# Differential attention scores from stacked high and low parts, second-map scaling on GpSimd, turned heads by transfers, and unread products in TensorE's waits

## The chip, the cores and the metric

One program runs on one core of a Trainium2 chip. The metric is the device time of one execution, in microseconds (us). The engines are named as the profile names them: PE is TensorE's products (PEld its weight loads), DVE is VectorE, ACT is ScalarE, POOL is GpSimd, SP is SyncE, which here only issues transfers. A q behind an engine's name is its sequencer.

## What is computed

Two transformer blocks over 512 tokens of 1024 features, with a small context of 256 tokens in the second. The first block has sliding-window attention with a pooled mixer, and a retrieval layer (PEER) over 16,384 experts. The second has two layers: differential attention with a SwiGLU feed-forward, then a short convolution with another. The change lies almost wholly in the differential attention, whose core is, for each of 8 heads with two maps each:

```
q, k = rope(rmsnorm(h @ wq)), rope(rmsnorm(h @ wk))   # 64 features per map; context keys without rope
s[m] = q[m] @ k[m].T / 8                              # two maps, 512 queries, 512 + 256 keys
p[m] = softmax(s[m])
o    = (p[0] - lam * p[1]) @ v                        # then an rmsnorm over 128 features, then w_o
```

rope's rotated copy exchanges neighbouring blocks of 16 features (`-x2, x1, -x4, x3`).

## The kernel before, in words

All weights pass through SBUF in units of 128x1024, in a ring of 8 slots: SP loads a unit (`load_unit`, L458), ACT writes its rounded high part (`split_hi`, L1147), POOL writes the rest as low part in four pieces of 256 columns (`low_part`, L535 to L540), and PE makes each fp32 product from three single-pass products (high by high, high by low, low by high: L639 to L641). Elsewhere, where both operands are plain fp32, one product takes two PE instructions. Every engine's work is written out in order by hand, with semaphores between engines, so the order of instructions in each engine's block is the schedule.

The stages around the change, in time order (the span starts at 0):

- Queries and keys, 1550 to 1683 us. For each of 16 own heads (8 of keys `Kd`, 8 of queries `Qd`, each 128 rows for two maps' halves) PE makes a unit's 24 products, ACT squares and copies the bank (`evict`, L1446), PE sums the squares (`head_squares`, L918), and PE turns the copy by a product with a 128x128 matrix (`rotate`, L926). DVE then runs `own_head` (L2104): turned times sine (L2111), straight times cosine and gain (L2112), their sum (L2113), a reciprocal of the root (L2102), a scaling (L2115). Four context items of keys lie between. ACT may run four items ahead of DVE.
- Values, 1681 to 1757 us: four pairs of value units, six products' groups each; the first two rounds' scores are put into the last pair.
- The rounds, 1757 to 1908 us: 32 rounds of one head and 128 queries. In round a PE makes the scores of round a + 2 (`at_scores`, L998, 64 rows by 128 queries by 512 and 256 keys, for two maps that lie in different halves of the rows), transposes round a (L1009) and multiplies values of the head before (L1018). DVE finds the maxima (`at_max`, L2131), ACT takes the exponentials with their sums (`at_exps`, L1499), DVE inverts the sums (`at_parts`, L2152, L2153), ACT scales the second map by -lam over its sum (`at_second`, L1505), DVE adds the first map to it (`at_combine`, L2158), PE transposes, ACT copies (L1542). Within DVE's round the order is `at_parts(a+1)`, two `at_max(a+2)`, `at_combine(a+1)`, then a head's odd work (L2164 on, L2186). One bank pair per map holds the scores, so scores wait for the exponentials of the round before. During these rounds POOL has nothing to do, and the first units of the output projection lie ready in the ring.
- The output projection from 1911 us, the first feed-forward to 2324 us, the convolution's norm (L1132) with PE waiting for DVE, and the rest to the end.

## Time and profile before

| | |
|---|---|
| median of 3 runs | 2876.49 us (2873.24 to 2891.11) |
| the profiled execution | 2884.48 us, of which the span of instructions is 2882.7 us |
| mean granted TensorE clock of the profiled execution | 0.992 |
| PE busy | 2806.1 us, 97% of the span |
| DVE, ACT, POOL busy | 1779.1, 982.2, 1611.1 us |

The span is what the rows below refer to; the execution has 1.8 us around it. PE is busy nearly throughout, but busy time is counted from each product's start to its modelled end, and products overlap, so a share near 1 does not say that products follow as fast as they can.

### The profile page before, as it was taken

What the parts mean: (1) busy time and instruction counts of PE and PEld (TensorE: products, weight loads), DVE (VectorE), ACT (ScalarE), POOL (GpSimd) and SP (SyncE); (2) the same over time, 40 slices, a digit from 0 to 9 for tenths busy, and PEclk for the clock granted to TensorE, in tenths of its full rate; (3) what the DMA queues carried; (4) which work ended last, traced back from release to release, by engine and by line L of the source; (5) the groups of instructions that cost most, each with busy time, mean ns of one, the idle gap of its engine ahead of it and who ended that gap; (6) DMA issues with size and microseconds to landing.
All of it is one profiled execution on the core that took longest, in us unless ns stands there. A gap on an engine that the chain in (4) does not pass through costs nothing.

```text
span 2882.7 us, 39051 instructions
## 1 busy us (share of the span) xinstructions
PE 2806.1 (97%) x14400; PEld 2399.9 (83%) x14400; DVE 1779.1 (62%) x2749; ACT 982.2 (34%) x1452; POOL 1611.1 (56%) x1649
## 2 busy tenths in 40 slices
PE   8799999999999999999999999999999989999999
PEld 6698888888888899999998786579888868988887
DVE  6668999997652378788887855754333353433333
ACT  4432333322223333333334446843122232332121
POOL 5444878787777357878741441016455545555543
PEclk9999999999999999999999999999999999999999
DMA  6932444489984699999993111003222222222221
GB/s 200 342 140 82 145 145 148 140 327 320 331 289 155 230 320 336 337 353 348 368 353 110 59 59 48 1 20 109 102 95 100 97 73 97 94 95 95 88 103 72
DMA packets 191668, 499.23 MB, mean 173 GB/s; under 512 B 29624, under 2 KB 80952, under 8 KB 190904
## 3 DMA queue, kind: packets, MB, share of 16 engines
q1 hardware_dynamic: 104528, 338.95, 33.8%
q10 hardware_dynamic: 52200, 91.23, 9.0%
q0 software_dynamic: 34816, 67.41, 6.6%
q8 instruction: 76, 1.25, 0.2%
q14 instruction: 48, 0.39, 0.0%
HBM read 432.82 MB, written 64.68 MB: 173 GB/s over the span
## 4 chain that ended last, share of the span: by engine, by line
PE 86%; POOL 5%; DVE 3%; DMA 2%; issue 2%; ACT 1%; SPq 0%; ACTq 0%; DVEq 0%
PE ps L639 27%; PE ps L641 26%; PE ps L640 26%; POOL value_rows L566 2%; POOL picked L558 2%; PE ps L998 2%; PE ps L1018 1%; DMA unit_raw<-w_units 1%; PE ps L1009 1%; DMA value_rows<-w_units,row_at 1%; PE ps L918 1%; PE ps L828 0%; PE ps L926 0%; DMA abuf<-act_dram 0%; DVE std L1624 0%
## 5 line engine op out<-in xcount | busy, mean ns | idle before, releaser
L540 POOL TENSOR_TENSOR unit_lo<-unit_raw,unit_hi 128x256 fp32r<-128x256 f32 x984 | 761.9, 811 | 939.0 <-ACT unit_hi L1155 938.4
L639 PE MATMUL ps<-hn_hi,unit_hi 128*128 128x512 f32 (+1 forms) x2352 | 910.8, 387 | 23.6 <-DVE hn_lo L1725 11.7
L640 PE MATMUL ps<-hn_lo,unit_hi 128*128 128x512 f32 (+1 forms) x2352 | 896.3, 381 | 0.0
L641 PE MATMUL ps<-hn_hi,unit_lo 128*128 128x512 f32 (+1 forms) x2352 | 896.3, 381 | 0.0
L1155 ACT ACTIVATE unit_hi<-unit_raw 128x1024 fp32r<-128x1024 f32 x486 | 506.0, 1055 | 459.4 <-DMA unit_raw<-w_units 359.7
L639 PEld LDWEIGHTS ps<-hn_hi,unit_hi 128*128 128x128 f32 x2352 | 443.1, 188 | 124.2 <-issue 14.5
L572 POOL DMA_INDIRECT gate_dram<-gate_sums,gate_at x384 | 468.6, 1220 | 136.9 <-issue 126.7
L640 PEld LDWEIGHTS ps<-hn_lo,unit_hi 128*128 128x128 f32 x2352 | 443.3, 188 | 87.1 <-issue 4.5
L641 PEld LDWEIGHTS ps<-hn_hi,unit_lo 128*128 128x128 f32 x2352 | 443.1, 188 | 85.2
L1857 DVE TENSOR_TENSOR unit_lo<-unit_raw,unit_hi 128x1024 fp32r<-128x1024 f32 x240 | 292.3, 1222 | 107.8 <-ACT unit_hi L1155 104.8
L639 PE MATMUL ps<-gp_hi,unit_hi 128*128 128x384 f32 x1024 | 345.5, 337 | 12.5 <-DVE gp_lo L2019 12.5
L641 PE MATMUL ps<-gp_hi,unit_lo 128*128 128x384 f32 x1024 | 344.1, 336 | 0.0
L640 PE MATMUL ps<-gp_lo,unit_hi 128*128 128x384 f32 x1024 | 343.9, 336 | 0.0
L2241 DVE TENSOR_TENSOR pf<-gel,ps 128x512 f32<-128x512 f32 x44 | 30.3, 688 | 379.7 <-PE ps L641 379.7
L1356 ACT ACTIVATE stage<-ps 128x512 f32<-128x512 f32 x128 | 76.6, 599 | 492.7 <-PE ps L641 492.7
L566 POOL DMA_INDIRECT value_rows<-w_units,row_at x128 | 188.0, 1469 | 100.6 <-DVE own_values L2037 60.5
L558 POOL DMA_INDIRECT picked<-act_dram,act_at x128 | 177.6, 1387 | 67.8 <-issue 38.7
L639 PEld LDWEIGHTS ps<-gp_hi,unit_hi 128*128 128x128 f32 x1024 | 193.8, 189 | 15.2 <-DVE gp_lo L2019 10.8
L1575 ACT ACTIVATE gel<-ps 128x512 f32<-128x512 f32 x44 | 26.4, 599 | 497.2 <-PE ps L641 497.2
L640 PEld LDWEIGHTS ps<-gp_lo,unit_hi 128*128 128x128 f32 x1024 | 193.8, 189 | 0.0
L641 PEld LDWEIGHTS ps<-gp_hi,unit_lo 128*128 128x128 f32 x1024 | 193.5, 189 | 0.0
L2037 DVE SCALAR_TENSOR_TENSOR own_values<-value_rows,picked,own_values 128x1024 f32<-128x1024 f32 x127 | 163.0, 1284 | 42.3 <-DMA value_rows<-w_units,row_at 40.2
(284 smaller groups left out, 3784.3 us busy)
## 6 DMA issues: line engine op xcount, KB each, us to landing
unit_raw<-w_units SPq DMA_DIRECT2D x486, 512.0 KB, 3.6
araw<-ada_units SPq DMA_DIRECT2D x96, 512.0 KB, 6.0
act_dram<-stage ACTq DMA_DIRECT2D x32, 1024.0 KB, 6.6
gate_dram<-zero SPq DMA_DIRECT2D x8, 3072.0 KB, 24.7
abuf<-act_dram ACTq DMA_DIRECT2D x32, 768.0 KB, 7.9
gbuf<-gate_dram ACTq DMA_DIRECT2D x15, 1536.0 KB, 21.2
gate_dram<-gate_sums,gate_at POOLq DMA_INDIRECT x384
x<-x_t SPq DMA_DIRECT2D x8, 256.0 KB, 6.4
```

The lines of the kernel that those rows point to most:

```text
L540: last = nc.gpsimd.tensor_tensor(lo[:, u % RING, cols], raw[:, u % RING, cols], hi[:, u % RING, cols].bitcast(F32), ALU.subtract)
L558: pool.indirect_dma_start(picked[:, k:k + 1], None, act_dram.rearrange("u j (t o) -> (u j t) o", o=1), bass.IndirectOffsetOnAxis(act_at[:, ...
L566: pool.indirect_dma_start(vrows[:, k % ROWS, :], None, w_units.rearrange("u p n -> (u p) n"), bass.IndirectOffsetOnAxis(row_at[:, k:k + 1] ...
L572: pool.indirect_dma_start(gate_dram.rearrange("i j (t o) -> (i j t) o", o=1), bass.IndirectOffsetOnAxis(gidx[:, t - 1, k:k + 1], 0), gsum[ ...
L639: mm(dst, wh, ah, start=start, stop=False)
L640: mm(dst, wh, al, start=False, stop=False)
L641: return mm(dst, wl, ah, start=False, stop=stop)
L998: last = mm(SD[m][:, keys], Qd[rows, 4 * m + h // 2, qt * P:(qt + 1) * P], Kd[rows, 4 * m + h // 2, keys], start=True, stop=True)
L1155: activation(hi[:, u % RING], raw[:, u % RING], ACT.Copy).then_inc(hi_ready, 1)
L1356: activation(stage[:, g % 2, u % BUNCH], ps[:, u % 4, :], ACT.Gelu).then_inc(gel_done, 1)
L1857: V.tensor_tensor(lo[:, u % RING], raw[:, u % RING], hi[:, u % RING].bitcast(F32), ALU.subtract).then_inc(value_lo_ready, 1)
L2037: last = V.scalar_tensor_tensor(own[:, :], vrows[:, k % ROWS, :], picked[:, k:k + 1], own[:, :], ALU.mult, ALU.add)
```

## The change

Seven edits:

1. `rotate` goes from PE. SP copies each evicted head's blocks of 16 rows into another buffer, exchanged, by 8 transfers of 16x512 (`turn_head`), and DVE's first step takes that buffer from SBUF with gain and signed sine (the sign now lies in the sine table). Items may run six ahead of DVE instead of four.
2. Scores are made from rounded parts. Per head and map ACT writes the high part of keys and queries (`high_keys`, `high_queries`); POOL writes the keys' low part into the other 64 rows, a second copy of the queries' high part into the other 64, and the queries' low part. One product of 128 rows and one of 64, both single-pass, then take the place of each fp32 product of 64 rows. Heads 0 and 1 are prepared during the values, the others during the rounds, two ahead.
3. `at_second` moves from ACT to POOL.
4. The parts lie in ring slots, so the output units load later: three after the scores of the sixth head, the others after all scores; their high and low parts are put into the last rounds and behind.
5. `keep_clock` issues products nobody reads: 9 ahead of the rounds, 3 in each of the first four rounds, 11 and 26 around the convolution's norm.
6. The load of x is waited for in three groups instead of eight pieces.
7. Buffers are moved to make room; the turning matrix leaves the constants.

```diff
 CTX_SQUARE = 112
+TURN = [(p + 16) % 32 for p in range(32)]
+X_GROUPS = (2, 3, 3)
...
         def pooled_bank(g):
             return ps[:, 4 if g == 3 else 5 + g, :]
+        def head_rows(h, m):
+            b = (h + m) % 2
+            return slice(64 * b, 64 * b + 64), slice(64 - 64 * b, 128 - 64 * b)
+        def key_parts(h, m):
+            return keyp[h // 2 % 2][:, 2 * (h % 2) + m, :]
+        def query_parts(h, m):
+            return qryp[h // 2 % 2][:, 4 * (h % 2) + m, :]
+        def query_low(h, m):
+            return qryp[h // 2 % 2][:, 2 + m, :]
         def seam_bank(k, j):
...
+        PARTS_AFTER = {0: (unit_used, U_DIFF + 2 * DC + 2), 1: (unit_used, U_DIFF + 2 * DC + 4),
+                       2: (unit_used, U_DIFF + 2 * DC + 6), 3: (unit_used, U_DIFF + 2 * DC + 6),
+                       4: (at_s, 2 * 2 * TT), 5: (at_s, 2 * 2 * TT), 6: (at_s, 4 * 2 * TT), 7: (at_s, 4 * 2 * TT)}
...
+                sp.wait_ge(hd_ev, upto("own", m))
+                if m == 0:
+                    sp.wait_ge(x_spilled, 16)
+                if m >= len(turnb):
+                    sp.wait_ge(hd_done, upto("own", m - len(turnb)))
+                for a in range(0, P, 32):
+                    for to, of in ((a, a + 16), (a + 16, a)):
+                        sp.dma_start(turnb[k][to:to + 16, :], src[of:of + 16]).then_inc(turn_in[k], 16)
             for n in range(2 * DC):
                 load_unit(U_DIFF + DC + n, of=U_DIFF + DC + (n + DC) % (2 * DC))
-            load_range(U_DIFF + 3 * DC, N_UNITS)
+                turn_head(n)
+            for n in range(DC):
+                if n == 0:
+                    sp.wait_ge(at_s, 6 * 2 * TT)
+                elif n == 3:
+                    sp.wait_ge(at_s, 8 * 2 * TT)
+                load_unit(U_WO + n)
+            load_range(U_WO + DC, N_UNITS)
             for c in range(DC):
                 sp.wait_ge(x_done, X_ALL - DC + c + 1)
...
+            def low_keys(h, m):
+                pool.wait_ge(head_high, 2 * h + 1)
+                own, other = head_rows(h, m)
+                summed(G_.tensor_tensor(key_parts(h, m)[other], Kd[own, 4 * m + h // 2, :],
+                                        key_parts(h, m)[own].bitcast(F32), ALU.subtract))
+            def high_again(h, m):
+                pool.wait_ge(head_high, 2 * h + 2)
+                own, other = head_rows(h, m)
+                summed(G_.tensor_copy(query_parts(h, m)[other], query_parts(h, m)[own].bitcast(F32)))
+            def low_queries(h, m):
+                own, _ = head_rows(h, m)
+                summed(G_.tensor_tensor(query_low(h, m)[own], Qd[own, 4 * m + h // 2, :],
+                                        query_parts(h, m)[own].bitcast(F32), ALU.subtract))
+                if m:
+                    G_.sem_inc(parted, 1)
+            def at_second(a):
+                pool.wait_ge(at_m, 3 * a + 3)
+                G_.tensor_scalar(Ed[a % 3][:, 1, :], Ed[a % 3][:, 1, :], stats[:, a % 2, 1, 3:4], None, ALU.mult)\
+                    .then_inc(at_scaled, 1)
+                pool.wait_ge(at_scaled, a + 1)
+            pool.wait_ge(lo_ready, U_PEER + LOW_FROM + U_WO - (U_DIFF + LAG))
+            for h in range(2):
+                for m in range(2):
+                    low_keys(h, m)
+                for m in range(2):
+                    high_again(h, m)
+                for m in range(2):
+                    low_queries(h, m)
+            at_second(0)
+            at_second(1)
+            for a in range(TT * HEADS):
+                if a + 2 < TT * HEADS:
+                    at_second(a + 2)
+                h, step = 2 + a // 4, a % 4
+                if h < HEADS:
+                    if step < 2:
+                        low_keys(h, step)
+                    elif step == 2:
+                        for m in range(2):
+                            high_again(h, m)
+                    else:
+                        for m in range(2):
+                            low_queries(h, m)
+                if 26 <= a < 29:
+                    low_part(U_WO + a - 26)
+            low_range(U_WO + 3, N_UNITS)
...
                 last.then_inc(unit_used, 1)
+            def keep_clock(u, bank, n):
+                s = u % RING
...
                     if a:
-                        pe.wait_ge(at_exp, 3 * (a - 1) + m + 1)
-                    rows = slice(64 * ((h + m) % 2), 64 * ((h + m) % 2) + 64)
+                        pe.wait_ge(at_exp, 2 * (a - 1) + m + 1)
+                    own, _ = head_rows(h, m)
                     for keys in (slice(0, T), slice(T, KEYS)):
-                        last = mm(SD[m][:, keys], Qd[rows, 4 * m + h // 2, qt * P:(qt + 1) * P],
-                                  Kd[rows, 4 * m + h // 2, keys], start=True, stop=True)
+                        mm(SD[m][:, keys], query_parts(h, m)[:, tok], key_parts(h, m)[:, keys], start=True, stop=False)
+                        last = mm(SD[m][:, keys], query_low(h, m)[own, tok], key_parts(h, m)[own, keys], start=False,
+                                  stop=True)
                     last.then_inc(at_s, 1)
...
             pe.wait_ge(v_ev, KTS * DC // 2)
+            keep_clock(U_WO - 1, 7, 9)
             for a in range(N_AT):
                 h, qt = a // TT, a % TT
                 if a + 2 < N_AT:
                     at_scores(a + 2)
                 at_transpose(a)
+                if h == 0:
+                    keep_clock(U_WO - 1, 7, 3)
                 if h and qt < 3:
                     at_values(h - 1, (2 * qt, 2 * qt + 1))
                 if h >= 2 and qt == 1:
...
+            unit_in(U_SC)
+            keep_clock(U_SC, 3, 11)
             norm(5)
+            keep_clock(U_SC, 3, 26)
             for j in range(DC):
                 if j >= 2:
...
-                    act.wait_ge(hd_done, i - 3)
+                if i >= len(nb):
+                    act.wait_ge(hd_done, i - len(nb) + 1)
...
+            def high_keys(h):
+                act.wait_ge(hd_done, upto("own", DC // 2 + h // 2))
+                act.wait_ge(*PARTS_AFTER[h])
+                for m in range(2):
+                    own, _ = head_rows(h, m)
+                    last = activation(key_parts(h, m)[own], Kd[own, 4 * m + h // 2, :], ACT.Copy)
+                last.then_inc(head_high, 1)
+            def high_queries(h):
+                act.wait_ge(hd_done, upto("own", DC + DC // 2 + h // 2))
+                for m in range(2):
+                    own, _ = head_rows(h, m)
+                    last = activation(query_parts(h, m)[own], Qd[own, 4 * m + h // 2, :], ACT.Copy)
+                last.then_inc(head_high, 1)
             for s in range(2 * DC):
...
+                    if n in (2, 4) and t == 0:
+                        act.wait_ge(hd_done, upto("own", 2 * DC - 3))
                     activation(Vd[n][:, t, :], ps[:, 6 + j % 2, 0:P], ACT.Copy)
                     activation(Vd[n + 1][:, t, :], ps[:, 6 + j % 2, P:2 * P], ACT.Copy).then_inc(v_ev, 1)
                     if t == 0:
                         behind_unit(2 * DC + n)
+                    if n in (2, 4) and t == 1:
+                        high_keys(n // 2 - 1)
+                        high_queries(n // 2 - 1)
+                    if n == DC - 2 and t == 2:
+                        high_keys(2)
                     if n == DC - 2 and t == 1:
                         at_exps(0)
-                    if n == DC - 2 and t == 3:
-                        at_second(0)
                 behind_unit(2 * DC + n + 1)
             at_exps(1)
-            at_second(1)
             for a in range(N_AT):
...
                 if h % 2 and h >= 3 and qt == 1:
                     at_roots(h - 3)
+                if qt == 1 and h + 2 < HEADS:
+                    high_queries(h + 2)
+                if qt == 3 and h + 3 < HEADS:
+                    high_keys(h + 3)
+                if 25 <= a < 28:
+                    split_hi(U_WO + a - 25)
                 if a == 2:
...
             at_roots(HEADS - 2)
+            for u in range(U_WO + 3, U_WO + AHEAD):
+                split_hi(u)
...
             def own_head(m):
                 i = upto("own", m) - 1
                 dst, g = (Kd[:, m, 0:T], pc("dk")) if m < DC else (Qd[:, m - DC, :], gain(8)[:, 0:1])
-                dve.wait_ge(hd_rot, m + 1)
+                k = m % len(turnb)
+                dve.wait_ge(turn_in[k], 128 * (m // len(turnb) + 1))
                 if i:
                     dve.wait_ge(hd_done, i)
-                V.tensor_tensor(rtmp[:, :], turn_bank(m), cs[:, 1], ALU.mult).then_inc(hd_turned, 1)
+                V.scalar_tensor_tensor(turnb[k][:, :], turnb[k][:, :], turns(m // DC), cs[:, 1], ALU.mult, ALU.mult)
                 link(V.scalar_tensor_tensor(dst, dst, g, cs[:, 0], ALU.mult, ALU.mult))
-                link(V.tensor_tensor(dst, dst, rtmp[:, :], ALU.add))
+                link(V.tensor_tensor(dst, dst, turnb[k][:, :], ALU.add))
                 head_inverse(i)
-                V.tensor_tensor(dst, dst, nb[:, i % 4, :], ALU.mult).then_inc(hd_done, 1)
+                V.tensor_tensor(dst, dst, nb[i % len(nb)][:, :], ALU.mult).then_inc(hd_done, 1)
             def context_heads(c):
...
-                dve.wait_ge(at_exp, 3 * a + 2)
+                dve.wait_ge(at_exp, 2 * a + 2)
                 link(V.reciprocal(st[:, :, 3], st[:, :, 2]))
                 V.tensor_scalar(st[:, 1, 3:4], st[:, 1, 3:4], lamt[:, 69:70], None, ALU.mult).then_inc(at_m, 1)
             def at_combine(a):
-                dve.wait_ge(at_exp, 3 * a + 3)
+                dve.wait_ge(at_scaled, a + 1)
                 V.scalar_tensor_tensor(Ed[a % 3][:, 0, :], Ed[a % 3][:, 0, :], stats[:, a % 2, 0, 3:4],
                                        Ed[a % 3][:, 1, :], ALU.mult, ALU.add).then_inc(at_p, 1)
```

## Rows read from the trace of the kernel before

**Rows 1.** The page: the span, and the chain that ended last by engine.

```profile
span 2882.7 us, 39051 instructions
...
PE 86%; POOL 5%; DVE 3%; DMA 2%; issue 2%; ACT 1%; SPq 0%; ACTq 0%; DVEq 0%
```

**Rows 2.** Windows: length, busy time of each engine, clock, DMA; queries and keys, the rounds.

```profile
core 0: us, PE busy (x) PEld busy (x) DVE busy (x) ACT busy (x) POOL busy (x), PEclk, DMA share, GB/s
1562.00:1683.00 121.00, 120.90 (x527) 90.59 (x527) 107.63 (x79) 61.92 (x96) 51.95 (x62) 1.00 0.22 73
...
1757.00:1908.00 151.00, 140.36 (x636) 81.31 (x637) 107.77 (x185) 118.94 (x204) 2.67 (x4) 0.95 0.06 21
```

**Rows 3.** Groups of PE instructions by line, 1550 to 1700 us: turning the keys.

```profile
L926 PE MATMUL ps<-Kd,rot_gains 128*128 128x512 f32 x16 | 8.2, 592 | 0.0
```

**Rows 4.** The chain in order of time: start, length, what.

```profile
1564.17 0.86 PE ps L926 x2
```

**Rows 5.** Timeline of DVE: the first own head's first step, the last one's last.

```profile
1565.17 0.69 DVE L2111 TENSOR_TENSOR rtmp<-ps,cs 128x512 f32<-128x512 f32 x1 [3.59 <-PE ps L926]
...
1695.37 0.69 DVE L2115 TENSOR_TENSOR Qd<-Qd,nb 128x512 f32<-128x512 f32 x1
```

**Rows 6.** Timeline of SP's queue at the start: issuing eight transfers.

```profile
2.13 4.88 SPq L485 DMA_DIRECT2D x<-x_t x8
```

**Rows 7.** Transfers by line: size, median us from issue to landing.

```profile
x<-x_t SPq DMA_DIRECT2D x8, 256.0 KB, 6.4
...
out_dram<-x SPq DMA_DIRECT2D x8, 256.0 KB, 2.0
```

**Rows 8.** Timeline of PE in three rounds.

```profile
1801.79 1.57 PE L998 MATMUL ps<-Kd,Qd 64*128 64x512 f32 x8
...
1804.00 1.88 PE L1018 MATMUL ps<-PTd,Vd 128*128 128x512 f32 x4
1805.81 2.11 PE L998 MATMUL ps<-Kd,Qd 64*128 64x512 f32 x8
...
1809.50 2.44 PE L998 MATMUL ps<-Kd,Qd 64*128 64x512 f32 x8 [0.78 <-ACT Ed L1499]
```

**Rows 9.** Timeline of ACT: first exponentials of rounds 2 and 31.

```profile
1761.64 0.90 ACT L1499 ACTIVATE Ed<-ps,stats 128x768 f32<-128x768 f32 x1 [1.64 <-DVE stats L2131]
...
1894.22 0.90 ACT L1499 ACTIVATE Ed<-ps,stats 128x768 f32<-128x768 f32 x1 [0.81 <-DVE stats L2131]
```

**Rows 10.** Groups of ACT instructions by line in the rounds, 1757 to 1908 us.

```profile
L1499 ACT ACTIVATE Ed<-ps,stats 128x768 f32<-128x768 f32 x62 | 55.4, 900 | 19.1 <-DVE stats L2131 19.1
L1505 ACT ACTIVATE Ed<-Ed,stats 128x768 f32<-128x768 f32 x31 | 29.1, 939 | 7.4 <-DVE stats L2153 7.4
```

**Rows 11.** Groups of DVE instructions by line in the rounds.

```profile
L2131 DVE TENSOR_REDUCE stats<-ps 128x1 f32<-128x768 f32 x60 | 55.0, 955 | 22.0 <-PE ps L998 21.9
L2158 DVE SCALAR_TENSOR_TENSOR Ed<-Ed,stats 128x768 f32<-128x768 f32 x31 | 31.3, 1009 | 1.0 <-ACT Ed L1505 1.0
L2153 DVE TENSOR_SCALAR stats<-stats,lamt 128x1 f32<-128x1 f32 x31 | 6.6, 214 | 1.1
```

**Rows 12.** Groups of POOL instructions by line, whole span.

```profile
L596 POOL TENSOR_SCALAR pool_tmp<-pool_tmp 128x496 f32<-128x496 f32 x2 | 2.9, 1456 | 0.1
L597 POOL TENSOR_TENSOR pool_p<-pool_tmp,pool_p 128x512 f32<-128x512 f32 x2 | 2.5, 1265 | 0.2
L593 POOL TENSOR_TENSOR pool_tmp<-pool_tmp 128x510 f32<-128x510 f32 x2 | 2.1, 1040 | 0.0
```

**Rows 13.** Timeline of POOL: a unit's four low pieces beside DVE's heads, and alone.

```profile
1660.68 3.87 POOL L540 TENSOR_TENSOR unit_lo<-unit_raw,unit_hi 128x256 fp32r<-128x256 f32 x4 [5.39 <-ACT unit_hi L1155]
...
1700.28 2.84 POOL L540 TENSOR_TENSOR unit_lo<-unit_raw,unit_hi 128x256 fp32r<-128x256 f32 x4 [9.91 <-ACT unit_hi L1155]
```

**Rows 14.** One line's instructions: min, median, max ns.

```profile
L2112 DVE SCALAR_TENSOR_TENSOR Qd<-Qd,gmod,cs x8: 741/936/1204, 1642.8 to 1690.5; 128x512 f32<-128x512 f32 x8
```

**Rows 15.** Windows: one in the rounds, one in the convolution's norm.

```profile
1828.00:1832.00 4.00, 4.00 (x16) 3.33 (x18) 2.68 (x4) 2.54 (x6) 0.00 (x0) 0.50 0.00 0
2330.00:2335.00 5.00, 0.42 (x1) 0.45 (x2) 4.80 (x5) 1.39 (x2) 0.00 (x0) 0.50 0.00 0
```

More of the change, by code:

```diff
@@ L99 @@
 CTX_SQUARE = 112
+TURN = [(p + 16) % 32 for p in range(32)]
+X_GROUPS = (2, 3, 3)
+X_GROUP = [k for k, n in enumerate(X_GROUPS) for _ in range(n)]
 FINAL = (6, 7, 0, 1, 2, 3, 4, 5)
@@ L277, in cc @@
             return con[:, o + a:o + a + (w - a if n is None else n)]
-        ident, blocks, ones, rot, iota = (cc(n) for n in ("ident", "blocks", "ones", "rot", "iota"))
+        ident, blocks, ones, iota = (cc(n) for n in ("ident", "blocks", "ones", "iota"))
         eps, epsd = cc("eps"), cc("epsd")
@@ L288, in gain, with turns @@
             return gmod[:, 8 * k:8 * k + 8]
+        def turns(which):
+            return gain(9)[:, 2 + which:3 + which]
         NORMS = [(x, T, pc("norm1"), None, hn_hi, hn_lo),
@@ L345, in build_program @@
         consts_in = sem("consts_in")
-        x_loaded, con2_in = [sem(f"x_loaded{c}") for c in range(DC)], sem("con2_in")
+        x_loaded, con2_in = [sem(f"x_loaded{c}") for c in range(len(X_GROUPS))], sem("con2_in")
         x_done = sem("x_done")
@@ L659, in project @@
                 last.then_inc(unit_used, 1)
+            def keep_clock(u, bank, n):
+                s = u % RING
+                for _ in range(n):
+                    mm(ps[:, bank, :], hi[:, s, 0:P], hi[:, s, 0:T], start=True, stop=True)
             def norm(k):
@@ L1045, in _ @@
                 if n == DC - 2:
-                    pe.wait_ge(hd_done, N_ITEMS)
                     at_scores(0)
@@ L1459, in evict @@
                 for to, of in moves:
-                    last = activation(nb[to, i % 4, :], ps[of, n % 2 if kind == "own" else 2 + n % 2, :], ACT.Square)
+                    last = activation(nb[i % len(nb)][to], ps[of, n % 2 if kind == "own" else 2 + n % 2, :], ACT.Square)
                 last.then_inc(hd_sq, 1)
@@ L2319, in constants @@
     put("ones", 1.0 / P)
-    turn = np.zeros((P, P))
-    for m in range(P):
-        if m % 32 < 16:
-            turn[m + 16, m] = -1.0
-        else:
-            turn[m - 16, m] = 1.0
-    put("rot", turn)
     put("iota", r[None, :])
```

63 lines of the change are left out of this document (28 added, 35 removed).

## The prediction

> **What bounds the kernel now.** I read the page first, then the windows of the stages that the change touches, then the lines and the timelines inside them. The chain that ended last lies 86% on PE [rows 1], so time is won only where PE, or what PE waits for, gets shorter. Two stages matter. In the queries and keys PE is busy 120.9 of 121 us, but DVE is busy 107.6 too, and its heads run from 1565.2 to 1696.1 us, 13 us past the end of PE's part [rows 2, 5]: DVE is the second bound, close behind. In the rounds PE is busy 140 of 151 us, ACT 119, DVE 108, POOL 2.7 [rows 2]. A round takes 4.57 us on the mean, from the first exponentials of round 2 at 1761.64 us to those of round 31 at 1894.22, over 29 rounds [rows 9]. Sometimes PE sets it (a round's scores start as soon as the values of the last are through), sometimes the ring of scores, maximum, exponentials, with PE idle before the scores (0.78 us in one row) [rows 8]. So no engine is far ahead of the others, and what a lighter PE gives there depends on which engine takes over.
>
> **The change part by part.**
>
> *Turning by transfers.* PE loses 32 instructions. A pair takes 0.86 us of the chain [rows 4] and there are 16 pairs (the row of keys has 16 instructions in 8.2 us, and the queries as many [rows 3]): 16 x 0.86 = 13.8 us less for PE. In return SP issues 8 transfers a head. Eight issues took 4.88 us [rows 6], and a landing took 2.0 us in one group and 6.4 in another, both of larger pieces [rows 7]; I take 2.5. So DVE has its first turned head about 4.9 + 2.5 us after the copy at about 1562.5, near 1570, some 5 us later than now, and 9 at the upper bound. SP's queue then holds 5 us of issues per head of 6 to 7 us, with the unit loads between; a unit load waits at most behind one head's transfers and is eight units ahead. DVE's first step becomes one of two SBUF inputs, 0.74 to 1.2 us instead of 0.69 [rows 5, 14]: 16 x 0.2 = 3 us. Against that DVE no longer waits for PE inside the stage, 11 us in 3 waits, as the first of 3.59 us shows [rows 5]; now it is behind from the start, and PE may run six items ahead. DVE therefore ends near 1570 + 126, at 1696, as now. PE reaches the values 13.8 us earlier, at about 1667, and the first thing there that wants DVE's last heads is an eviction at about 1687, for the third last head, due at about 1682. The margin is 5 us; if transfers land late it is gone and up to 5 us are given back. I take -13.8, bounds -14 and -8.
>
> *Scores.* The old products are only 64 rows high and the two maps lie in different halves of the rows. When both are free to go, eight instructions take 1.57 us, and one waiting for the other map 2.11 or 2.44 [rows 8]. The new ones fill all 128 rows, so the maps can't lie side by side. Per map there are two products over 512 and two over 256 columns, single-pass. Four 512-column products of the two-pass kind take 1.88 us [rows 8], so a map's (3 such lengths) costs at most 1.4 us, and 0.65 if a single pass runs twice as fast as half of an old one. I take 1.3 us for both maps. That is 0.3 to 1.1 us less for PE in a round, and no halving.
>
> *What POOL gets.* Per head and four rounds: four scalings of 128x768 with one input, two subtractions over 768 columns, two copies and two subtractions over 512. The one long scaling by a constant in the trace is 496 columns in 1.456 us [rows 12]; by columns 768 would be 2.25, and with a fixed start somewhat less: 2.2. Subtractions at 1.265 for 512 columns give 1.9 for 768 [rows 12]; no long copy is there, and I put it below the addition of 1.04, at 0.9. Sum: 4 x 2.2 + 2 x 1.9 + 2 x 0.9 + 2 x 1.27 = 16.9 us a head. POOL and DVE slow each other where DVE reads two SBUF inputs: four low pieces took 3.87 us beside two such steps of DVE and 2.84 alone [rows 13], about 0.5 per step, and the DVE step went from 0.74 to as much as 1.2 us [rows 14]. `at_combine` is such a step, one per round: 4 x 0.5 more. So POOL needs 18.9 us for a head, **4.75 us a round**, which is more than the 4.57 of today. It is behind a second wait too: `at_combine` waits for POOL, and queued behind it on DVE are the inversion and the maxima of the next rounds, for which ACT and then PE wait. That loop is the inversion with its scaling, 0.4 (0.214 for the second [rows 11]; the one ahead is as short), POOL 2.2, `at_combine` 1.0 alone and 1.5 beside POOL's next step [rows 11, 14], a head's odd work 0.3 to 0.6 and two handovers: 4.5 to 4.9. Both say the same.
>
> Beside a measured 2.2 us per scaling stands a page: the Trainium skill, "GPSIMD Engine Reference", 4.1 Engine selection, says that a GpSimd operation with one input runs at roughly line rate. Then 768 columns would cost below 1 us, an estimate from that page of the Trainium skill. The row here (1.456 us for 496 columns, longer than an addition of two inputs over 510) speaks against it [rows 12].
>
> *What ACT loses and gets.* It loses 0.94 us a round [rows 10] and gets, per head, two copies of 64x768 and two of 64x512: at the same 0.94 for 768 columns and about 0.6 for 512, 3.1 us a head, 0.8 a round. ACT is where it was.
>
> *The rounds, summed.* 24 rounds carry a step of the parts: 24 x 4.75 = 114.0. Three carry a low part of an output unit instead: 2.2 + 2.84 + 0.5 = 5.5 each, 16.6. Two carry neither: 0.4 + 2.2 + 1.0 + 0.6 = 4.2, 8.4. Sum 139.0 against the 132.6 of rows 9, +6.4. PE then stands idle about a sixth of a round, and where PE was held up the clock has fallen: it was at 0.50, the level of 1.2 GHz, for the window at 1828, when PE had just waited for exponentials [rows 15]. At that level four us hold two us of work. I add 4 us for two or three more such stretches (0 to 12). So +10.4.
>
> *The small ones.* Two rounds' scores among the values: -0.5. Nine unread products ahead of the rounds: at most 9 x 0.47 by the four products of rows 8, I take 2, and 2 back for a clock that stays up (0 to 3). The three per round in the first head run while PE would wait. Around the convolution's norm PE is idle anyway, 0.42 of 5 us busy at a clock of 0.50 [rows 15]; the first products behind it come at DVE's pace, so a full clock gives 0 to 1 us: 0. The late output units: three come during the rounds (counted), five after the last scores, with 25 us to the output projection (their lows at 2.84 each [rows 13] are ahead of PE): 0, and up to 3 if not. The load of x in groups: the copies that wait longer stand in front of a wait for the second unit: 0, up to 0.5.
>
> Sum: -13.8 + 10.4 - 0.5 = -3.9. Against the profiled execution's 2884.5 that is 2880.6; the median of the runs shown is 8.0 lower, and I forecast by it: 2876.5 - 3.9 = **2872.6**.
>
> **The rivals.**
>
> *POOL is quick.* If a scaling goes at the rate of the additions, 1.04 x 768 / 510 = 1.57 us [rows 12], or less, POOL needs 4 us a round at most, and ACT (two exponentials with their sums 2.0, a copy 0.8, the parts 0.8, odd work and table loads 0.5) and PE hold the round at about 4.2: 29 x 4.2 + 4 = 126, -6.8. Time 2876.5 - 13.8 - 6.8 - 0.5 = 2855. For it speaks that the long scalings of the trace are only two; against it, that both took the same 1.456 us. By the line rate of the Trainium skill the time would be this one too, since ACT and PE then hold the round.
>
> *The clock falls through the rounds: slower.* PE has about 4 us of work in a round of 4.75, and fewer in a head's last round, without values. If PE drops to 1.2 GHz in more than about 15 of the rounds, a round there takes up to 8 us at half rate; at +2.7 each on the mean, 15 rounds are +40: 2872.6 + 40 = 2913. It decides from some 13 such rounds on (35 us). For it: the window at 1828 [rows 15]. Against: the mean clock is 0.95 over the rounds although PE waits in many [rows 2].
>
> *POOL is slowed throughout.* If all POOL work pays 1.36 (3.87 over 2.84 [rows 13]), a head takes 23 us, 5.75 a round: 24 us more, 2897.
>
> *The turning is not won.* If transfers come late or DVE ends 8 us later, PE waits among the values: 2881.
>
> **How the numbers follow.** Forecast 0.45, POOL quick 0.25, clock 0.12, POOL slowed 0.10, turning not won 0.08. The range that leaves out no more than 2 in 10 goes from a quick POOL with every small bound (2855 less 6) to the slowed POOL with one stretch of low clock (2897 + 9): 2849 to 2906. Within 1% (28.8 us, about what a measurement of this kernel can tell from no change) lie 2848 to 2905. Faster by over 1% needs a POOL quicker than the quick case, and all of the clock: 0.14. Slower by over 1% is the clock case and a part of the slowed POOL: 0.14. The rest, 0.72, is within 1%.
>
> **What would show it.** The turned product gone from PE and the values starting 12 to 14 us earlier; DVE's heads ending near 1696. In the rounds POOL busy above 85% for the first 24, DVE's longest wait the one of `at_combine` for POOL, scalings of 2.2 us, and first exponentials 4.7 to 4.8 us apart. ACT and PE with more idle time than now. I am wrong if POOL's scaling is well off 2.2 us in either direction, if PE's clock is below 0.9 over the rounds, or if PE waits for DVE's evictions among the values.

## The result and the profile after

The changed kernel takes 2894.5 us (median of 20 runs, 2883.4 to 2910.7), beside 2880.3 us for the kernel before on the same chip (20 runs). The ratio, with its 95% interval, is 1.0050 [1.0033, 1.0068]: 14 us slower, where 4 us less had been forecast. The profiled execution after has a span of 2893.5 us, 10.8 more than the one before; page and windows first, which answer to [rows 1, 2].

```profile
span 2893.5 us, 39382 instructions
...
PE 84%; POOL 7%; DVE 4%; DMA 2%; issue 2%; ACT 1%; SPq 0%; POOLq 0%; ACTq 0%; DVEq 0%
```

```profile
core 0: us, PE busy (x) PEld busy (x) DVE busy (x) ACT busy (x) POOL busy (x), PEclk, DMA share, GB/s
1562.00:1683.00 121.00, 120.70 (x613) 98.26 (x611) 113.23 (x82) 65.44 (x108) 55.46 (x68) 1.00 0.36 102
1757.00:1908.00 151.00, 147.96 (x563) 83.83 (x562) 115.16 (x167) 101.87 (x180) 133.74 (x76) 0.99 0.09 33
2330.00:2345.00 15.00, 14.82 (x63) 11.40 (x62) 12.79 (x16) 6.62 (x11) 2.46 (x3) 1.00 0.19 71
```

In the rounds POOL has gone from 2.7 to 133.7 us of 151, PE from 140.4 to 148.0, and the clock is 0.99, higher than before. So PE has no more slack there than it had, although its work was to become lighter. Where the time went is read from ScalarE's timeline, first exponentials of rounds 2 and 31 (answers to [rows 9]):

```profile
1748.67 0.90 ACT L1621 ACTIVATE Ed<-ps,stats 128x768 f32<-128x768 f32 x1 [2.85 <-DVE stats L2259]
...
1901.89 0.90 ACT L1621 ACTIVATE Ed<-ps,stats 128x768 f32<-128x768 f32 x1 [3.10 <-DVE stats L2259]
```

The rounds take 1901.9 - 1748.7 = 153.2 us, 5.28 each, against 132.6 and 4.57: **20.6 us more**. They start 13.0 us earlier: 2.4 of that was there before ScalarE's first step on the queries and keys (at 1559.0 us instead of 1561.4), 12.0 come from the turning, and 1.4 are lost again among the values. Behind the rounds 3.0 us more are lost up to the first output projection product, which starts at 1921.95 us instead of 1911.27. From there to the end it is 971.6 us after and 971.4 before: -13.0 + 20.6 + 3.0 + 0.2 = +10.8, the whole difference of the spans.

Who paces the rounds? First GpSimd, its groups over 1690 to 1925 us, and then its timeline beside VectorE's in one round:

```profile
L698 POOL TENSOR_SCALAR Ed<-Ed,stats 128x768 f32<-128x768 f32 x32 | 70.5, 2204 | 45.9 <-DVE stats L2281 44.4 <-POOL query_parts L690 0.2
L678 POOL TENSOR_TENSOR key_parts<-Kd,key_parts 64x768 fp32r<-64x768 f32 x16 | 38.8, 2427 | 10.6 <-ACT key_parts L1589 9.3
L690 POOL TENSOR_TENSOR query_parts<-Qd,query_parts 64x512 fp32r<-64x512 f32 x16 | 25.4, 1589 | 1.3
...
L685 POOL CAST query_parts<-query_parts 64x512 fp32r<-64x512 f32 x16 | 13.4, 838 | 1.0
```

```profile
1829.73 2.21 POOL L698 TENSOR_SCALAR Ed<-Ed,stats 128x768 f32<-128x768 f32 x1 [0.69 <-DVE stats L2281]
1832.02 3.51 POOL L690 TENSOR_TENSOR query_parts<-Qd,query_parts 64x512 fp32r<-64x512 f32 x2
1837.16 2.20 POOL L698 TENSOR_SCALAR Ed<-Ed,stats 128x768 f32<-128x768 f32 x1 [1.64 <-DVE stats L2281]
1839.45 2.64 POOL L678 TENSOR_TENSOR key_parts<-Kd,key_parts 64x768 fp32r<-64x768 f32 x1
```

```profile
1831.97 1.02 DVE L2286 SCALAR_TENSOR_TENSOR Ed<-Ed,stats 128x768 f32<-128x768 f32 x1 [0.33 <-POOL Ed L698]
1832.91 1.50 DVE L2296 TENSOR_SCALAR ob<-Od 128x512 f32<-128x512 f32 x1
1834.44 1.64 DVE L2297 TENSOR_TENSOR ob<-ob 128x512 f32<-128x512 f32 x1
1836.00 0.74 DVE L2314 SCALAR_TENSOR_TENSOR Od<-Od,gmod,ps 128x512 f32<-128x512 f32 x1
1836.66 0.16 DVE L2280 RECIPROCAL stats<-stats 128x2 f32<-128x2 f32 x1
1836.85 0.21 DVE L2281 TENSOR_SCALAR stats<-stats,lamt 128x1 f32<-128x1 f32 x1
```

Read these as a chain: scaling, then `at_combine` 0.03 us later, then `at_square` (1.50 + 1.64 us here; 0.42 + 0.69 in the kernel before, rows below), `at_scale` (0.74 us, the norm's gain), the inversion, and only then the next scaling, for which GpSimd stands still 1.64 us. This round is 7.43 us long from scaling to scaling.

```profile
L2169 DVE TENSOR_TENSOR ob<-ob 128x512 f32<-128x512 f32 x7 | 4.8, 693 | 0.2
L2168 DVE TENSOR_SCALAR ob<-Od 128x512 f32<-128x512 f32 x7 | 3.0, 422 | 0.0
```

Now PE, one map's scores and the rest of a round (answers to [rows 8]; L1096 has 128 rows, L1097 has 64):

```profile
1776.93 0.49 PE L1096 MATMUL ps<-key_parts,query_parts 128*128 128x512 f32 x1
1777.35 0.50 PE L1097 MATMUL ps<-key_parts,query_parts 64*128 64x512 f32 x1
1777.78 0.39 PE L1096 MATMUL ps<-key_parts,query_parts 128*128 128x256 f32 x1
1778.10 0.38 PE L1097 MATMUL ps<-key_parts,query_parts 64*128 64x256 f32 x1
1778.41 0.87 PE L1108 MATMUL ps<-con,Ed 128*128 128x128 f32 x6
1779.12 1.88 PE L1117 MATMUL ps<-PTd,Vd 128*128 128x512 f32 x4
...
1783.69 0.55 PE L1108 MATMUL ps<-con,Ed 128*128 128x128 f32 x3
```

Starts are what counts, since ends are modelled. They lie 0.42 us apart at 512 columns and 0.31 at 256, so one map takes 1.48 us and both 2.96. From transposes to transposes a round with values and without a wait is 1783.69 - 1778.41 = 5.28 us on PE. That this is also the mean round is chance: the next round, a head's last, has no values and takes 3.76 us, one that carries the norm's sums takes 6.18, and from 1787.45 to 1807.96 us four rounds of PE take 20.5, 5.13 each. PE's waits from 1757 to 1908 us (us in all, how many, the longest):

```profile
PE ps L1096 <- ACT Ed L1621: 2.1, 2, 1.1
```

PE stands idle for 2.1 of the 153.2 us, so as the kernel stands PE sets the rounds. Whether GpSimd's chain would hold them as long without PE this profile can't say. So there are two candidates for the pace, and they lie on top of each other.

### The profile page after: what moved, and what is told of

Its sections match the earlier page's. It is cut to its first block, busy times and chain, and to the rows that moved or that the text cites. A ratio compares the mean times of both kernels' runs of the same rounds, so it can differ in the third digit from the quotient of the medians.

```text
span 2893.5 us, 39382 instructions
## 1 busy us (share of the span) xinstructions
PE 2836.1 (98%) x14426; PEld 2422.1 (84%) x14426; DVE 1799.2 (62%) x2751; ACT 977.9 (34%) x1452; POOL 1759.2 (61%) x1729
## 4 chain that ended last, share of the span: by engine, by line
PE 84%; POOL 7%; DVE 4%; DMA 2%; issue 2%; ACT 1%; SPq 0%; POOLq 0%; ACTq 0%; DVEq 0%
PE ps L740 27%; PE ps L742 26%; PE ps L741 26%; POOL value_rows L610 2%; POOL picked L602 2%; POOL Ed L698 1%; DMA unit_raw<-w_units 1%; DMA value_rows<-w_units,row_at 1%; PE ps L1097 1%; PE ps L1096 1%; PE ps L1025 1%; PE ps L935 0%; DMA abuf<-act_dram 0%; POOL unit_lo L584 0%; PE ps L1117 0%
## 5 line engine op out<-in xcount | busy, mean ns | idle before, releaser
L740 PE MATMUL ps<-hn_hi,unit_hi 128*128 128x512 f32 (+1 forms) x2352 | 910.2, 387 | 17.6 <-DVE hn_lo L1851 10.2
```

Of the source, the lines that this page charges most:

```text
L740: mm(dst, wh, ah, start=start, stop=False)
```

## Experiments

All ratios are to the kernel before on the same chip. The rounds are the time from the first exponentials of round 2 to those of round 31, read as above from one profiled execution of each run; PE idle and the granted clock are those of the same stretch. In these executions the first copy of a key head lies anywhere from 1546.0 to 1574.1 us, so their whole times aren't compared. The theory at the start was the prediction's own (GpSimd's loop sets the rounds); the rival was PE's products.

| run | scaling on | score products | rounds us | each | PE idle us | clock | ratio [95%] |
|---|---|---|---|---|---|---|---|
| before | ScalarE | old | 132.6 | 4.57 | 8.4 | 0.96 | 1 |
| changed | GpSimd | 128 and 64 rows in turn | 153.2 | 5.28 | 2.1 | 0.99 | 1.0050 [1.0033, 1.0068] |
| e1 | ScalarE | in turn | 158.3 | 5.46 | 2.6 | 0.96 | 1.0075 [1.0051, 1.0099] |
| e5 | GpSimd | 128 rows first | 152.1 | 5.24 | 12.2 | 0.93 | 1.0038 [1.0019, 1.0057] |
| e6 | GpSimd | both 128 rows | 151.6 | 5.23 | 30.5 | 0.95 | 1.0028 [1.0001, 1.0055] |
| e7 | GpSimd | only the 128 rows | 151.5 | 5.23 | 37.1 | 0.88 | 1.0017 [0.9995, 1.0039] |
| e8 | GpSimd | old, parts still made | 153.8 | 5.30 | 17.9 | 0.93 | 1.0022 [1.0003, 1.0042] |
| e12 | ScalarE | 128 rows first | 142.7 | 4.92 | 10.1 | 0.96 | 0.9997 [0.9972, 1.0021] |
| e9 | ScalarE | both 128 rows | 131.4 | 4.53 | 17.5 | 0.97 | 0.9945 [0.9923, 0.9967] |
| e13 | GpSimd | both 128 rows, small squares | 146.4 | 5.05 | 28.4 | 0.98 | 0.9999 [0.9980, 1.0017] |
| e15 | GpSimd | in turn, small squares | 152.7 | 5.26 | 0.0 | 0.97 | 1.0055 [1.0034, 1.0076] |
| e2 | ScalarE | old, no parts | 133.5 | 4.60 | 7.8 | 0.95 | 0.9947 [0.9925, 0.9969] |
| e10 | GpSimd | old, no parts | 129.5 | 4.47 | 6.1 | 0.98 | 0.9949 [0.9923, 0.9975] |

### The pieces by themselves

**e1, scaling back on ScalarE.**

```diff
-                G_.tensor_scalar(Ed[a % 3][:, 1, :], Ed[a % 3][:, 1, :], stats[:, a % 2, 1, 3:4], None, ALU.mult)\
-                    .then_inc(at_scaled, 1)
...
+                activation(Ed[a % 3][:, 1, :], Ed[a % 3][:, 1, :], ACT.Copy, scale=stats[:, a % 2, 1, 3:4])\
+                    .then_inc(at_scaled, 1)
```

> The changed kernel with the second map's scaling back on ACT; the parts of the scores stay on POOL. Theory A (the rounds are set by the loop from DVE's inversion over POOL's scaling and POOL's next step back to DVE): a round falls from 5.28 us to 4.3 to 4.5, some 25 us less than the changed kernel, ratio to the kernel before 0.996. Theory B (the rounds are longer because of the parts themselves, ACT's and POOL's copies and the new products; the scaling is hidden): rounds stay near 5.2, ratio 1.005.

Measured: 1.0075, rounds of 5.46 us. Its window of the rounds:

```profile
1757.00:1908.00 151.00, 148.53 (x546) 84.53 (x546) 104.20 (x162) 120.69 (x199) 53.72 (x44) 0.95 0.08 29
```

GpSimd is now 54 us busy and PE 148.5 of 151. The theory that GpSimd's loop alone makes the rounds long falls: with that loop gone, PE, idle for 2.6 us, keeps them as long. The 5.1 us over the changed kernel fit the fall of the granted clock: at the lower level, 1.2 GHz, PE takes twice as long (value products start 0.85 us apart there in e5, 0.43 at the full clock), so (1 - 0.957) x 158.3 = 6.8 us are lost here and (1 - 0.989) x 153.2 = 1.7 there, an estimate from the two clocks.

**e2, the turning alone**, put into the kernel before (with x loaded in three groups, which frees the semaphores):

```diff
-                    rotate(s - 1)
...
+                turn_head(n)
```

> The kernel before with the turning by transfers alone (and the load of x waited for in three groups). Theory A and B: the values start 12 us earlier, the rounds stay at 4.57 us, ratio 0.996. If the turning were given back among the values (late transfers, DVE behind): 0.999 to 1.000.

Measured: 0.9947, so 15 us won. **e3** is the reverse, the changed kernel with the old turning.

> The changed kernel with the turning undone (PE turns the heads again). If the turning is worth its 12 us there too: ratio 1.009. If its gain is lost behind slower rounds that do not care when they start: 1.005.

Measured: 1.0090 [1.0064, 1.0116], 12 us over the changed kernel, with the same rounds (153.5 us). By the ratios the turning is worth 12 to 15 us in either surrounding. The traces are sharper: from the first copy of a key head to the first eviction of the values it is 121.7 us in the two kernels that turn on PE (before, e3) and 109.7 in all the others, so 12.0 us.

**e4, without the unread products** (`keep_clock` loops over `range(0)`).

> The changed kernel without the products that nobody reads. If they only fill waits: same time as the changed kernel, ratio 1.005. If they keep the clock up: more windows at a clock of 0.50 at the start of the rounds and in the convolution's norm, 2 to 6 us more, ratio 1.006 to 1.007. If they stand in the way: 1.004.

Measured: 1.0058 [1.0033, 1.0083], which the interval can't tell from the changed kernel's. In the profiled execution the first rounds ran at a clock of 0.54 (window 1738 to 1771 us) against 0.95 with the products (1748 to 1782), and the rounds took 168.6 us; the runs' times don't show such a loss on the mean. **e11** adds the products to e2:

> The kernel before with the turning by transfers (x in three groups) and the unread products (9 ahead of the rounds, 3 in each of the first four, 11 and 26 around the norm), old score products, scaling on ScalarE. The turning alone gave 0.9947. Theory E (the granted clock dips in the first rounds and around the norm cost 2 to 6 us and the unread products remove them): ratio 0.992 to 0.994. Rival F (PE sets these rounds, so that 12 products of 0.23 us cost 2.8 us there and the dips only move): ratio 0.995 to 0.996.

Measured: 0.9936 [0.9913, 0.9958], beside 0.9947. These two comparisons have the same sign, as has e14 against e10 below; each interval reaches over the difference, so neither a gain nor its size is settled.

### Two limits side by side

After e1 the theory was that each change between a 128-row and a 64-row product exposes a load of weights of 0.19 us. **e5** has half the changes:

```diff
                     for keys in (slice(0, T), slice(T, KEYS)):
                         mm(SD[m][:, keys], query_parts(h, m)[:, tok], key_parts(h, m)[:, keys], start=True, stop=False)
+                    for keys in (slice(0, T), slice(T, KEYS)):
                         last = mm(SD[m][:, keys], query_low(h, m)[own, tok], key_parts(h, m)[own, keys], start=False,
```

> The changed kernel with each map's four score products in another order: both 128-row products first (512 and 256 columns), then both 64-row ones, so that the row shape changes half as often. Theory A (at each change between a 128-row and a 64-row product the next load of weights, 0.18 to 0.19 us in the trace, is no longer hidden under the product before: 0.227 + 0.19 = 0.42 us at 512 columns, 0.12 + 0.19 = 0.31 at 256, as the starts stand): four of the eight such gaps go, PE's scores fall from 2.95 to about 2.2 us a round, and the rounds from 5.28 us to the 4.7 to 4.95 of GpSimd's loop (140 to 147 us for exponentials 2 to 31 instead of 153). Time 6 to 12 us under the changed kernel, ratio to the kernel before 1.001 to 1.003. Rival B (these products run at the two-pass rate of the value products, 0.43 us at 512 columns, in any order): rounds stay at 5.3, ratio 1.005. Rival C (GpSimd's loop sets the rounds): rounds stay at 5.1 to 5.3, ratio 1.004 to 1.005.

**e6** has none: `query_low(h, m)[own, tok], key_parts(h, m)[own, keys]` becomes `query_parts(h, m)[:, tok], key_parts(h, m)[:, keys]`.

> The changed kernel with the second product of each pair made 128 rows high as well: it multiplies the same operands as the first once more, so the scores are doubled and the low part of the queries is left out. Only the row shape differs, the columns streamed stay. Theory A: no gap for a load of weights is left, scores 1.4 us a round on PE (0.227 at 512 columns, 0.12 at 256), PE has slack, and the rounds are GpSimd's: 4.65 to 4.95 us, 138 to 147 us in all, ratio 1.000 to 1.003, and PE's granted clock may fall. Rival B (two-pass rate): starts stay 0.43 apart, rounds 5.3, ratio 1.005. Rival C (GpSimd): rounds 5.1 to 5.3 although PE waits.

**e7** drops the second product, **e8** uses `Qd` and `Kd` as before the change.

> The changed kernel without the 64-row products: the scores lack the low part of the queries times the high part of the keys. GpSimd's and ScalarE's steps all stay. Theory A: scores 0.7 us a round on PE, less if anything than with two 128-row products, but the rounds are then GpSimd's, 4.65 to 4.95 us: the same time as with both at 128 rows within 4 us, ratio 1.000 to 1.003. Rival B: scores 1.4 to 1.5 us a round, rounds at GpSimd's 4.65 to 4.95 as well; B is told from A by the starts here, 0.43 and 0.31 us apart against 0.23 and 0.12. Rival C: 5.1 to 5.3.

> The changed kernel with the old score products (full precision, 64 rows, on the keys and queries themselves), while the parts are still made on ScalarE and GpSimd and the scaling stays on GpSimd. Theory A: scores back at 1.57 to 2.44 us a round on PE, two maps side by side; PE needs 4.1 to 4.9 us a round, and the rounds are set by GpSimd's 4.65 to 4.95: 140 to 147 us, ratio 1.001 to 1.003, so the new products were worth less than nothing. Rival C (GpSimd's loop, with its steps slowed beside VectorE, makes the rounds long): rounds stay at 5.1 to 5.3 us, ratio 1.004 to 1.005.

PE's timeline of e6, one map:

```profile
1776.29 0.50 PE L1096 MATMUL ps<-key_parts,query_parts 128*128 128x512 f32 x1
1776.63 0.40 PE L1097 MATMUL ps<-key_parts,query_parts 128*128 128x512 f32 x1
1776.86 0.28 PE L1096 MATMUL ps<-key_parts,query_parts 128*128 128x256 f32 x1
1776.98 0.28 PE L1097 MATMUL ps<-key_parts,query_parts 128*128 128x256 f32 x1
```

Four equal shapes stream the same columns in about 0.8 us instead of 1.48, with starts down to 0.23 and 0.12 apart: the gap belongs to the change of row shape (theory A), not to the rate of these products (rival B). Its size fits too: at those distances a map's four products take 0.70 us, four changes at 0.19 make that 1.46 (1.48 measured) and two make it 1.08, which is what a map takes in e12 below, a run with e5's order. But the rounds hardly moved: 151.5 to 153.8 us in all four, although PE idles for 12 to 37 us in them. In e6 GpSimd's rows of the same round are like the ones seen above:

```profile
1822.35 2.20 POOL L698 TENSOR_SCALAR Ed<-Ed,stats 128x768 f32<-128x768 f32 x1 [0.68 <-DVE stats L2281]
1824.63 3.52 POOL L690 TENSOR_TENSOR query_parts<-Qd,query_parts 64x512 fp32r<-64x512 f32 x2
1829.79 2.21 POOL L698 TENSOR_SCALAR Ed<-Ed,stats 128x768 f32<-128x768 f32 x1 [1.64 <-DVE stats L2281]
```

Scaling to scaling 7.44 us, as with the slow products. So rival C, GpSimd's chain, holds here, and A's forecast of 4.65 to 4.95 us a round was wrong. PE is idle for 30.5 us in e6, its clock over 1757 to 1900 us is 0.94 (0.87 in e7), and the rounds are no longer for it: the fall of the clock, a rival of the prediction, came and cost nothing that these rounds show.

If both limits are real, taking both away must give what neither gives alone. **e9** is e6 with e1's edit, **e12** is e5 with e1's edit, **e10** is e2 with the scaling on GpSimd.

> The changed kernel with both suspected limits taken away at once: the second product is 128 rows high too (the first one's operands again, so the low part of the queries is left out and the scores are doubled), and the scaling of the second map is back on ScalarE. Theory A2 (two limits stand side by side, PE with its gaps for loads of weights at 5.2 to 5.3 us a round, GpSimd's chain of scaling and parts at 5.1, so that taking away one alone gave nothing): rounds 4.3 to 4.6 us, 130 to 139 us for exponentials 2 to 31, time as with the turning alone within 8 us, ratio 0.994 to 0.998. Rival D (whenever PE gets slack here its granted clock falls and eats the slack): rounds stay at 4.9 or more, clock of the rounds 0.85 to 0.95, ratio 1.001 or more.

> The changed kernel with the score products in the order of two 128-row, then two 64-row ones, and the scaling of the second map back on ScalarE; nothing is left out. Theory A2: scores 2.1 to 2.2 us a round on PE, rounds 4.6 to 4.95 us, between the old products (4.57) and the changed kernel's (5.28): 139 to 149 us, ratio 0.997 to 1.001. Rival D: clock below 0.95 in the rounds and 5.0 us or more a round, ratio 1.003 or more.

> The kernel before with the turning by transfers (x in three groups) and the scaling of the second map on GpSimd, with the old score products; no parts, no unread products, and five low parts of the output units ahead of or between the scalings. Theory A2: GpSimd has 2.2 us of work in a round of 4.2 to 4.6, so it bounds nothing; ScalarE is relieved of 0.9 us a round, and PE's 4.2 to 4.4 us set the rounds: 131 to 138 us, ratio 0.993 to 0.997, equal to the turning alone. Rival C (a scaling of 2.2 us on GpSimd between exponentials and combine is itself too late in the chain): rounds 4.8 or more, 145 us or more, ratio 0.999 or more. No gain over the turning alone means that the relief of ScalarE is worth nothing, since PE sets these rounds.

Windows over the rounds of e9 and of e10, one fence each:

```profile
1734.00:1865.00 131.00, 113.51 (x566) 82.14 (x565) 103.45 (x171) 123.96 (x212) 54.12 (x46) 0.97 0.07 23
```

```profile
1733.00:1862.00 129.00, 122.85 (x561) 69.84 (x560) 100.68 (x171) 82.95 (x158) 67.10 (x34) 0.98 0.03 11
```

e9's rounds fall to 131.4 us and the time to 0.9945; e12, with half of the gaps left, lies between at 142.7. From e1 to e12 to e9 only the score products differ: 5.46, 4.92, 4.53 us a round. That is at least the price of the row changes: in e9 ScalarE is busy 124 of 131 us and PE waits 14.8 us for its exponentials, so another limit already hides a part. e10, a little below the forecast of 131, shows that the scaling on GpSimd does no harm by itself: without the parts GpSimd is 67 of 129 us busy, and the rounds are the shortest of the table. e9 shows the same of the parts, with the scaling on ScalarE. It is scaling and parts together, on one queue, that bind.

### Where in GpSimd's chain

**e13** takes e6 and shrinks `at_square`'s two steps, from the second head on, to 8 columns; **e15** does so with the products as changed.

```diff
-                link(V.tensor_scalar(ob[:, :], Od[h][:, :], ROOT_BIG, -ROOT_BIG, ALU.min, ALU.max))
+                n = T if h == 0 else 8
+                link(V.tensor_scalar(ob[:, 0:n], Od[h][:, 0:n], ROOT_BIG, -ROOT_BIG, ALU.min, ALU.max))
...
```

> The kernel with both score products 128 rows high (scores doubled, low part of the queries left out; PE has slack, rounds were 151.6 us), and from the second head on the output norm's two square steps on VectorE over 8 columns in place of 512, so that the norm's means come from old values. Theory G (the squares, slowed beside GpSimd to 1.50 + 1.64 us, hold up the inversion and with it GpSimd's next scaling): the one round per head of 6.8 to 7.4 us falls to about 5.0, five or six times in the stage: 9 to 13 us off, 139 to 143 us, ratio 0.998 to 1.000. Rival H (GpSimd's own steps, slowed beside VectorE, make the length): 148 to 151.6 us, ratio 1.002 to 1.003.

> The changed kernel with the same small squares (the norm's means come from old values), its score products as they are. Theory G with PE's limit right behind: GpSimd's chain gets 9 to 13 us shorter, but PE with 2.95 us of scores a round needs 5.0 to 5.3 us itself, so that the rounds stay at 148 to 153 us: ratio 1.003 to 1.005. Rival (PE's limit lies well below, and the long rounds of the run with the scaling on ScalarE came from its low clock): rounds 140 to 146 us, ratio 0.999 to 1.002.

e13's rounds take 146.4 us, 5.2 less than e6's: between theory G (139 to 143) and rival H (148 and more). Why no more is in VectorE's rows of e13:

```profile
1845.76 1.02 DVE L2286 SCALAR_TENSOR_TENSOR Ed<-Ed,stats 128x768 f32<-128x768 f32 x1 [0.75 <-POOL Ed L698]
1846.69 1.25 DVE L2297 TENSOR_SCALAR ob<-Od 128x8 f32<-128x8 f32 x1
1847.97 0.17 DVE L2298 TENSOR_TENSOR ob<-ob 128x8 f32<-128x8 f32 x1
```

Eight columns still take 1.25 us beside a GpSimd subtraction, against 0.17 in the next row. The step isn't slow, it is held until GpSimd's instruction has gone by: that subtraction runs from 1845.81 to 1847.91 us, and the step ends at 1847.94. So the squares account for 5 us at least. Of the 146.4 us left GpSimd is busy 132.6, subtractions that are held in their turn included (2.64 us for one of keys), and the rest is waiting. That rest wasn't split further. In e15 the rounds stay at 152.7 us, with PE 130.00 of 130 us busy in the window from 1790 and idle nowhere in the rounds: PE's limit is right behind, as expected, and below it a shorter chain is worth nothing.

### The version that the runs point to

**e14** is e10 with the unread products.

> Turning by transfers, scaling of the second map on GpSimd, the unread products, and the old score products; no parts. The turning with the scaling gave 0.9949, the turning with the unread products 0.9936. If both gains are real and add, 0.992 to 0.994; if PE sets these rounds whichever of the two is added, 0.9935 to 0.9955.

Measured: 2857.5 us, ratio 0.9916 [0.9896, 0.9937], rounds of 127.8 us (4.41 each): by the ratios 24 us faster than the kernel before and some 38 faster than the changed one. It drops the stacked parts and keeps the rest.

## Why the prediction was wrong

The forecast was 4 us faster and the time is 14 us slower. Most of the miss lies in one term: the rounds, put at 139.0 us and 4 for the clock, took 153.2. That is 10.2 us; the spans show 3.0 more behind the rounds, 1.9 among the values (1.4 lost, where 0.5 was to be won) and 1.8 in the turning. Two steps failed, and each alone would have made the rounds longer than forecast.

- **The step that failed** is the loop over GpSimd, "4.5 to 4.9. Both say the same." Where PE has slack (e6, e7) it holds the rounds at 5.23 us; in the changed kernel it is 5.28 over all rounds, and 5.53 from the scaling at 1807.62 us to the fourth behind it at 1829.73. The sum of GpSimd's own work was nearly right: 4 x 2.2 + 2 x 2.65 + 0.6 + 1.2 + 3.5 = 19.4 us a head in the rounds, for 18.9 forecast. Wrong was a chain in which "a head's odd work" on VectorE was put at 0.3 to 0.6 us. As a mean over four rounds that fits the undisturbed steps, (0.42 + 0.69 + 0.74) / 4 = 0.46, but they stand whole in one round: there it is 1.50 + 1.64 + 0.74 us between `at_combine` and the inversion. The contention had been charged to GpSimd's steps and to `at_combine`, but not to `at_square`, which stands in the same place and pays most. The loop's printed terms also add up to 3.9 to 4.7 without the two handovers, for which no figure stood.
- **A second step failed behind it:** "I take 1.3 us for both maps". They take 2.96, so "0.3 to 1.1 us less for PE in a round" became more, and PE, which was to stand idle a sixth of a round, is idle 2.1 us of all of them and sets them. What is missing is the price of changing between 128 and 64 rows, 0.19 us eight times a round. The upper bound that stood beside it, 1.4 us a map from the two-pass products, came near the 1.48 by luck, since two passes aren't what takes the time (e6: 0.8 us). This alone would have given nearly the same rounds: e1 and e15 are slow with GpSimd relieved or its chain shortened. So the sum needed both steps right; one would not have saved it.
- *Scaling at 2.2 us:* the prediction calls it measured, but it was worked out from the row of 496 columns; it is right, 2204 ns over 32, also in e10. That settles the rival of a quick GpSimd; by the Trainium skill, "GPSIMD Engine Reference", 4.1 Engine selection, one input would go at roughly line rate, and the trace, with those 2204 ns, doesn't agree.
- *POOL slowed throughout, 2897:* the nearest rival in time. Its mechanism is half right: the subtractions, a part of the copies and VectorE's squares were held. The scalings kept 2.20 to 2.21 us, but none of them ran beside a VectorE step other than the maxima over PSUM, so nothing here shows what such a step would do to them.
- *Turning by transfers, -13.8:* right in its mechanism, and 12.0 us in size. In the changed kernel the first value eviction starts at 1669.3 us instead of 1683.6, of which 2.4 were ahead; e2 and e3 give 15 and 12 us. VectorE's steps there took as much as 1.0 to 1.2 us beside GpSimd. It waited for a transfer only once, 7.4 us before the first head, and its last own head's last step starts at 1691.3 us instead of 1695.4 [rows 5].
- *The clock, +4 and the rival of 2913:* in the changed kernel the clock of the rounds rose to 0.99, with PE idle only 2.1 us. Where runs gave PE slack (e6, e7), it fell, in rounds that something else paced. Slack isn't all of it: in e15 PE is idle nowhere in the rounds and the clock is 0.97, and in e1 the fall cost time. Why it falls there no run shows.
- *Unread products and the norm:* around the convolution's norm the clock went from 0.50 [rows 15] to 1.00, and the time from the first output projection product to the end stayed, 971.4 and 971.6 us (972.2 in e4, without these products): forecast at 0 and right. In the rounds a gain is possible, not shown.
- *The late output units,* 0 to 3 us: the 3.0 us lost behind the rounds lie where they would, but no run separated them from the last scalings.

## What to carry to other kernels

When work moves to another engine, follow the whole cycle (who waits for the moved step, what is queued behind that wait, who needs that), and charge the contention of a shared path to every instruction inside it, not to the two that were compared. Two limits of the same length hide each other: undoing either alone showed nothing or a loss, and only a table with both factors did. A profile shows the first of them, by the engine that doesn't idle, and not the one behind it. And of products price the starts in their real order of shapes, not the columns.

## What the runs showed of the hardware

- Loads of weights of 0.18 to 0.19 us are hidden behind the product before when both have the same rows (starts 0.23 and 0.12 us apart in e6, 0.23 in the units), and when 128 and 64 rows alternate the starts lie 0.19 us further apart (0.42 and 0.31), as if a load stood fully between products. That it is the load, and not another cost of the change, is argued from the equal size. The Trainium skill, "TensorE: Matmul & The Clock Gate", Part 3 (The mechanism), says in its list that a load overlaps with running products only when the row groups differ, and ahead of the list that one into a background buffer is pulled ahead too. Here equal row groups overlap, so the measurement decides against the list's sentence for these shapes; which buffer a load takes, no run shows.
- GpSimd's two-input steps and VectorE's steps between SBUF tensors hold each other, for about a whole instruction: 0.42 us became 1.50, eight columns took 1.25 us, a subtraction of 768 columns went from 1.83 us at its shortest to 2.65 behind an `at_combine` of 1.02. VectorE's maxima over PSUM (0.95 us) and GpSimd's scaling (2.20 us) kept their times beside each other. The Trainium skill, "GPSIMD Engine Reference", 1. Specifications, says that the SBUF interfaces are shared, with contention from VectorE instructions that have two SBUF inputs or run in a 2-port mode. For two inputs the trace agrees and adds the sizes; the first step of `at_square` has one input, and no row shows its mode. Mostly the one that starts first keeps its time, but not always: beside GpSimd's copies it was `at_combine` that went to 1.45 us.
